# Scoring the whole K cache during the attention layer's projections, with the sample's queries made first

## What is computed

```
def fox_attend(q, cq, qpos, k, ck, kpos, v):
    s = jnp.einsum('bqhd,bkhd->bhqk', qb, k) * scale
    s = s + cq[..., :, None] - ck[:, :, None, :]        # sums of log forget values
    s = jnp.where(kpos[None, :] <= qpb[:, None], s, -jnp.inf)
    return jnp.einsum('bhqk,bkhd->bqhd', jax.nn.softmax(s, axis=-1), v)

def fox_sample(h, ck_pool, cv_pool, cl_pool, page_table, w_in, b_f, w_out):
    q, k, v, z, logf = fox_project(h, w_in, b_f)
    kp = ck_pool[page_table]                            # 8 x 4096 rows of 16 heads x 64
    vp = cv_pool[page_table]
    o = fox_attend(q, c_new, qpos, concat(kp, k), concat(c_past, c_new), kpos, concat(vp, v))
    return (o * silu(z)) @ w_out, k, v, logf
```

## Time and profile before

| | |
|---|---|
| median of 3 runs | 2210.48 us (2210.18 to 2215.91) |
| the profiled execution, its own time | 2207.72 us |
| its span | 2206.0 us |
| busy share of the span | PE 85%, PEld 61%, DVE 51%, POOL 28%, ACT 24% |
| moved by DMA | 384.64 MB, 174 GB/s over the span |
| layer 0 and `norm(1)` | 0 to 779 us |
| forget tile and 32 projection tiles | 779 to 1199 us |
| change of block and pass 0 | 1199 to 1321 us |
| passes 1 to 7 | 1321 to 2059 us |
| final stage | 2059 to 2206 us |

### The profile page before, as it was taken

The page is one execution under the profiler, slowest core; times in us unless marked ns, Lnnn a source line. Parts: engine busy times, 40 slices in busy tenths (PEclk is TensorE's granted clock), DMA queues, the critical chain, the costliest instruction groups (busy, mean ns, idle before and its releaser), DMA issues. The chain is left out here.

```text
span 2206.0 us, 36290 instructions
## 1 busy us (share of the span) xinstructions
PE 1884.8 (85%) x13168; PEld 1343.1 (61%) x13168; DVE 1126.3 (51%) x1846; ACT 538.1 (24%) x1203; POOL 610.2 (28%) x691
## 2 busy tenths in 40 slices
PE   4999999999999799999997568776777786778797
PEld 3877777787787677887886244443444443434475
DVE  4444444454464561112231676766676767676523
ACT  4211211121121332112111123232323232323421
POOL 0000000000000001001001676665666665666010
PEclk9999999999999999999998679898988898989899
DMA  4111111111111213223225779999999999999861
GB/s 139 39 45 48 36 49 48 40 50 43 40 41 48 97 58 102 93 76 97 93 76 138 268 221 342 348 342 330 336 362 329 352 325 330 339 344 337 294 220 59
DMA packets 184781, 384.64 MB, mean 174 GB/s; under 512 B 21009, under 2 KB 99250, under 8 KB 184366
## 3 DMA queue, kind: packets, MB, share of 16 engines
q1 hardware_dynamic: 126796, 196.59, 26.3%
q0 software_dynamic: 57376, 185.06, 25.0%
q10 hardware_dynamic: 466, 0.88, 0.1%
HBM read 353.94 MB, written 29.22 MB: 174 GB/s over the span
## 5 line engine op out<-in xcount | busy, mean ns | idle before, releaser
L332 POOL DMA_INDIRECT k_raw<-in_cache_k_dram,k_idx x512 | 496.3, 969 | 285.4 <-DVE kt L1525 140.9
L1525 DVE STREAM_TRANSPOSE kt<-k_raw 128x1024 f32<-128x1024 f32 x256 | 315.0, 1237 | 108.3 <-DMA k_raw<-in_cache_k_dram,k_idx 106.6
L876 DVE TENSOR_TENSOR w_lo<-w_raw,w_hi 128x1024 fp32r<-128x1024 f32 x96 | 109.0, 1135 | 332.9 <-ACT w_hi L516 330.3
L673 PE MATMUL ps_a<-h_hi,w_hi 128*128 128x512 f32 x656 | 263.6, 402 | 0.0
L675 PE MATMUL ps_a<-h_hi,w_lo 128*128 128x512 f32 x656 | 258.6, 394 | 0.0
L674 PE MATMUL ps_a<-h_lo,w_hi 128*128 128x512 f32 x656 | 258.6, 394 | 0.0
L1273 PE MATMUL b<-con,p_p 128*128 128x128 f32 x432 | 89.2, 322 | 134.8 <-DVE p_p L1539 91.4
L425 POOL DMA_DIRECT2D out_dram<-g_out x4 | 2.2, 543 | 628.7 <-ACT g_out L563 628.7
L1273 PEld LDWEIGHTS b<-con,p_p 128*128 128x128 f32 x432 | 52.3, 155 | 177.7 <-DVE p_p L1539 77.9
L1251 PE MATMUL b<-kt,q_bd 128*32 128x256 f32 x2048 | 139.8, 419 | 19.7 <-DVE q_n L1550 19.5
L673 PE MATMUL ps_b<-h_hi,w_hi 128*128 128x512 f32 x384 | 153.0, 398 | 0.0
(11 more groups left out here) (295 smaller groups left out, 3135.5 us busy)
## 6 DMA issues: line engine op xcount, KB each, us to landing
v_pg<-in_cache_v_dram SPq DMA_DIRECT2D x256, 512.0 KB, 6.4
w_raw<-in_w_in_pool_dram SPq DMA_DIRECT2D x32, 512.0 KB, 4.0
w_raw<-in_w_in_attn_dram SPq DMA_DIRECT2D x32, 512.0 KB, 4.3
w_raw<-in_w_out_pool_dram SPq DMA_DIRECT2D x16, 512.0 KB, 3.6
k_raw<-in_cache_k_dram,k_idx POOLq DMA_INDIRECT x512
d_sb<-decay POOLq DMA_DIRECT2D x32, 256.0 KB, 7.7
qa<-q_aug POOLq DMA_DIRECT2D x8, 528.0 KB
ka<-k_aug POOLq DMA_DIRECT2D x8, 528.0 KB
```

The source lines that it names most:

```text
L332: pool.indirect_dma_start(k_raw[:, k, i, :], None, cache_rows, bass.IndirectOffsetOnAxis(ap=row, axis=0)).then_inc(k_full[k], 16)
L673: nc.tensor.matmul(ps, ah, bh, start=j == 0, stop=False)
L876: V.tensor_tensor(w_lo[slot][:, 0:width], raw[:, 0:width], w_hi[slot][:, 0:width].bitcast(F32), ALU.subtract).then_inc(dve_lo, 1)
L1525: V.transpose(kt[s % 2][:, :, 64 * k:64 * k + 64].rearrange("p i (t c) -> p t i c", c=32), k_raw[:, k, :, :].rearrange("p t (i c) -> p t i ...
```

## The change

All K scoring moves from the second block into the first, behind the projection tiles.

- The queries of the samples are made ahead of everything else in the layer's projections: 4 MB of weight rows (`wq`, eight loads on SP) and 16 matmuls of 512 columns in plain float32 (L862 of the new file), a copy by ACT, 8 small folds, and one scaled copy into `q_s`. The Q tiles no longer have a `sample_tile`.
- A unit is now 4 pages with all heads: 4 indirect DMAs of 128 rows of 4 KB (`k_quad`), four transposing instructions, 32 matmuls of 128 columns. There are still 64 units of 2 MB. Tile (f, n) is followed by the units 8f + 2n and 8f + 2n + 1. `k_raw` has 4 slots, `kt` 2 units, as before; the scores have one PSUM bank (`b5`).
- ACT copies each unit's scores out of PSUM and stores them in DRAM (`unit_out`, `s_scr`, 131 KB a unit). In the passes POOL loads them again beside the decay (`score_half`), and DVE adds the terms once per two slots.
- Z no longer stays in SBUF during the projections: it is stored (`z_scr`) and loaded in the second block. All stores of the projections move from POOL's queue to SP's; POOL's queue holds the K loads.
- The transposes of K and V for the outputs are split, four after the first half of a tile's matmuls and four after the second, in one bank (`b4`).
- The Q, K and V of head pair 0 and the first 8 pages of V are loaded before the first block ends.
- The passes lose `sample_scores` on PE, `k_turn` and the `q_bd` copies on DVE, and the K loads on POOL. The rest of a slot stands as it did.

```diff
+        def k_quad(pool, u):
+            for k in range(4):
+                if u:
+                    pool.wait_ge(dve_kt, 4 * (u - 1) + k + 1)
+                pool.indirect_dma_start(k_raw[:, k, :], None, cache_rows,
+                                        bass.IndirectOffsetOnAxis(ap=k_idx[:, u, k:k + 1], axis=0)).then_inc(k_full[k], 16)
...
+                pool.wait_ge(pe_pre, 1)
+                pool.wait_ge(dve_ix, 1)
+                for u in range(UNITS):
...
+                    k_quad(pool, u)
...
+                def unit_out(b, s):
+                    u = b * QUADS + s
+                    act.wait_ge(pe_qk, u + 1)
+                    past(act, st_s[s % 2], b * (8 * QUADS) + 16 * (s // 2))
+                    nc.scalar.copy(ss_st[s % 2][:, :, :].rearrange("p h k -> p (h k)"), b5[:, 0:2 * PAGE]).then_inc(act_su, 1)
...
+                def unit_scores(b, s):
+                    if s == 0:
+                        pe.wait_ge(dve_q, b + 1)
+                    past(pe, act_su, b * QUADS + s)
+                    pe.wait_ge(dve_kt, b * (4 * QUADS) + (4 * s + 4))
+                    for hh in range(2):
+                        for j in range(4):
+                            for cg in range(4):
+                                i = 16 * hh + 4 * cg + j
+                                mm = nc.tensor.matmul(b5[32 * cg:32 * cg + 32, PAGE * hh:PAGE * hh + PAGE], q_bd[:, i, :],
+                                                      kt[s % 2][:, i, :], start=j == 0, stop=j == 3, tile_position=(0, 32 * cg))
+                    mm.then_inc(pe_qk, 1)
...
+                        half_tile(0, ps, slot, h_hi, h_lo, KT8)
+                        if n >= 2:
+                            row_turn(f, n, 0, more)
+                        half_tile(1, ps, slot, h_hi, h_lo, KT8).then_inc(tile_done, 1)
...
+                        if n >= 2:
+                            row_turn(f, n, 1, more)
+                        unit_scores(f, 2 * n)
+                        unit_scores(f, 2 * n + 1)
...
+                def k_turn(u):
+                    if u >= 2:
+                        dve.wait_ge(pe_qk, u - 1)
+                    for k in range(4):
+                        dve.wait_ge(k_full[k], 16 * (u + 1))
+                        V.transpose(kt[u % 2][:, :, 32 * k:32 * k + 32],
+                                    k_raw[:, k, :].rearrange("p (i c) -> p i c", c=32)).then_inc(dve_kt, 1)
...
+                        for j in range(2):
+                            if n >= 2:
+                                rows_copy(f, n, j)
+                            u = QUADS * f + 2 * n + j + 2
+                            if u < UNITS:
+                                k_turn(u)
+                            if n == 3 and j == 0 and f < KT8 - 1:
+                                unit_queries(f + 1)
...
-                        sample_scores(b, s)
                         if sample and s % 2 == 0:
                             sample_turn(b, s // 2)
...
-                        if ahead:
-                            k_turn(*ahead, 0)
                         prompt_norm(b, s, 0)
-                        if ahead:
-                            k_turn(*ahead, 1)
                         prompt_norm(b, s, 1)
-                        sample_scores(b, s, sample)
+                        if s % 2 == 0:
+                            sample_scores(b, s // 2, sample)
```

689 lines of the change are left out of this document (385 added, 304 removed).

## The result

The changed kernel takes **2301.37 us** (median of 4 runs, 2295.74 to 2306.33), the kernel before, beside it on the same chip, 2213.19 us (2210.18 to 2219.15). The ratio is 1.039, 95% interval 1.036 to 1.043: **slower by 88 us**, where 51 us less were forecast. The time lies outside the range and on its other side. The profiled execution has a span of 2294.0 us.

What follows compares the result with a forecast made beforehand. PE was taken to bound the projections and DMA the passes. Terms of +178, -58, -171 and nothing for the final stage sum to -51 us, forecasting 2158 us; the 8-in-10 range was 2100 to 2235.

Steps and rivals of the forecast that it cites:

- Term 1: Projections, first block: longer by about 178 us, mainly from eight score units added to each pass of four tiles.
- A pass is 70.7 us: Projections: four tiles with their eight added units take 70.7 us instead of 50.9, at 2.28 us per unit.
- I take it as just hidden: Projections: K's stream and other DMA traffic fit barely within the 70.7 us pass; 36 us kept for the range.
- The five amounts listed there: DMA bytes per projection pass: K 16.8 MB, weights 2.1, stores 3.2, scores 1.1, forget terms 0.7; summed as 23.3.
- the first rival: Projections: K's stream sets the pace, late transposes delaying the weight split; 2194 us, or 2235 at 290 GB/s; chance 0.17.
- Term 2: Change of block and pass 0: 64 us instead of 122, shorter by 58 us.
- the barrier with the small load, about 4 us: Change of block: PE's remaining stand for the barrier and a 128 KB load, about 4 us, bounds 2 and 10.2.
- Term 3: Passes 1 to 7, -171 us: 105.4 to 81.0 each, taking off units 16.7, slot 3 5.7, slot 5 1.7, among others.
- Of the 7.76 us for Q and K 6.8: Each pass's end: 6.8 of 7.76 us waiting for next Q and K goes, with POOL's queue freed and DMA slack.
- About 3 us of matmuls that ran at the low clock: Passes 1 to 7: about 3 us per pass saved on matmuls slowed by the low clock behind waits.
- The units covered the softmax: +9.5: Passes 1 to 7: without units covering them, softmax waits add 9.5 us per pass, bounds 0 and 15.4.
- The second rival: Passes stay 88 us through bare softmax chains and a half-rate clock; 2207 us, no change; chance 0.10.

Runs made afterwards that it cites:

- the run above: Kernel before with one K load, its score units left out too (one of 16 matmuls stays, transposes become one-column copies): 2049.78 us, ratio 0.928.

## Why the prediction was wrong

**What bounds the kernel** was read rightly: PE the projections, DMA the passes. The trade was seen as well. What failed is the price of both halves.

**Term 1** (+178, measured +232). "A pass is 70.7 us" was too much for PE's own work: a unit takes 1.95 us, the low bound, not 2.28, and a plain pass with nothing late 66.6. That is 33 us less in eight passes, of which the units explain 21; the rest wasn't traced. The one-off work around it (forget terms, and what DVE does between) cost 35 us instead of 14: eight passes of 66.6 less the 12 us of matmuls ahead of the first unit are 521, and the run with one K load has 556. DVE's order has a part in it: three times PE waits 5.6 to 5.7 us for a turn that needs a row copy, with K loaded once too. And "I take it as just hidden" was wrong by 65 us. (The five amounts listed there add up to 23.9 MB and not 23.3; at 339 GB/s that is 70.5 us of 70.7, no slack at all.) This is the first rival's effect: it asked for 302 GB/s or less, and the stage ran at 296. But that rate is what the stalls left, not what set the pace, and the rival's mechanism as written (a late transpose delays the weight split) isn't what happened: PE waited 2 us for weights. DVE's row copies stood behind the transposes, PE stood before its units, and the stream was stopped by that. With the order mended the rate is 325 GB/s, and only 11 us of the 65 remain. DVE's busy time had been added up (11 to 16 of 17.7 us: "it fits, and its order is the risk"), but the order was not walked through against PE's tile. What was taken there from the Trainium skill, "DMA: Bandwidth & Descriptors", section "Queues, rings and completion order", changed nothing, as said: no weight tile was late enough for PE to wait more than those 2 us. The landing that was estimated from it can't be read from the changed kernel's trace.

**Term 2** (-58, measured -30). The step "the barrier with the small load, about 4 us" left out what SP does ahead of the barrier: eight V page loads of 1 us of issue each, behind the last unit, then four stores. The gap was 18.9 us. Pass 0, put at 54 us as a pass without its sample work, took 73 at a clock of 0.64; the forecast had it at the clock of the other passes. 59 of the 73 us PE was busy, 14 it was idle. Pass 0 took 83 to 85 us in the runs that shortened the gap without filler, but 76 to 80 in five that left it alone, so part of that loss isn't the gap's.

**Term 3** (-171, measured -111). Passes 1 to 6, whose ends can be compared, take 106.7 us before (PE busy 81.0, idle 25.7) and 90.9 now (busy 68.3, idle 22.6). That is 15.7 us off each, where the forecast takes off 24.4.
- "Of the 7.76 us for Q and K 6.8": wrong. The wait was 8.5 us on average and is 7.9. The load takes 14 to 16 us from issue to landing, and only 8.2 us of work are left when its columns come free. POOL's queue had nothing to do with it: POOL stands and waits for PE's last scores (247 us in six passes). In the window above all DMA engines are busy while it lands, at 240 GB/s. Besides, the 7.76 us row was an "issue" one, the loop's turn. Missing: 6.2 us per pass.
- "About 3 us of matmuls that ran at the low clock" go: wrong in sign. The clock fell from 0.88 to 0.83, and PE's busy time fell by 12.7 us where the forecast's terms (16.7, 1.7 and 3.0) take off 21.4. Missing: 8.7 us. Filler brought the clock to 0.96, then to 1.00.
- "The units covered the softmax: +9.5": the net was close and the reason wrong, which is luck. 16.7 off and 9.5 back is 7.2 us; the units were worth 7.8. But what came back did not come as softmax waits. The forecast has them grow by 3.8 us (9.5 less the 5.7 of slot 3); they fell by 2.4, from 17.2 to 14.8. It came as slower matmuls: without the units PE's other work took 5.7 us more, in the run above, at the lower clock. This term was 6.2 us too high.

Together 6.2 + 8.7 - 6.2 = 8.7, the difference between 24.4 and 15.7.

The second rival, "the passes stay long", gave 88 us by a bare softmax and a low clock and had a chance of 0.10. Its clock came, its bare softmax didn't, and the wait for Q and K, which it let go, stayed. It was named for no change, and the first rival for 36 us, or 77 at 290 GB/s; that both came at once was not among the cases, and the range ended at 2235. The Trainium skill, "TensorE: Matmul & The Clock Gate", section "HAM oscillation — how this bites in real kernels", tells of a kernel whose DMA wait in each turn of its loop brought PE back to the half rate every time. The trace agrees for the waits for Q and K: 0.50 behind each of the six, for 9 to 29 us, and 1.00 in passes 1 to 6 once those waits were gone and others filled.

**Not settled:** what the 8 us at the turn of PE's loop are in the kernel before. The trace names nothing; they went when the loop was written out, and the changed kernel's shorter loop doesn't show them. Why pass 0 ran at 0.64 in the changed kernel and at 0.52 to 0.61 in most of the runs on it wasn't tried. Nor was filler in the kernel before with one K load, which would show whether the stream or something else kept it from paying there.

## What to carry to other kernels

Moving work off a stage that a stream bounds gives back only what stood on that stage's path: ask of each moved matmul whether it was standing in a wait, and whether it kept the clock up. Here PE lost 16 us per pass in one place to win 8 in the other. Where a stream passes through few buffers, walk one tile through the consumer's order, instruction by instruction: an engine whose busy time fits can still stop the stream by one copy of 0.7 us in the wrong place. And read a wait's length against the load's own time from issue to landing; a wait that a full loop turn lies beside is not worth what its row says.

## What the runs showed of the hardware

- Useless matmuls in waits shortened the changed kernel's passes: 22 of them (14.7 us) took a pass from 90.9 to 85.2 us and the clock from 0.83 to 0.96; with 19 (12.9 us) and the Q and K wait gone, 84.8 us at 0.85 fell to 78.8 at 1.00. In the kernel before, with the stream as bound, 12 of them (8.5 us) lengthened the kernel by 16 us.
- PE stood 5 to 8 us at the turn of a loop whose body has 838 matmuls in the trace, behind nothing visible, and not at all with 582 or with the loop written out.
- A load of 1.08 MB in two issues took 14 to 16 us to land, in the window above with the DMA engines at a share of 1.00, moving 240 GB/s; K's stream at a share of 0.95 to 0.96 moved 324 to 325.
